# Two layers of product-key experts on one core: a tile's u rows are requested ahead of the preceding tile's v rows

## The reference

```
def peer_ffn(tokens, wq, sub_keys, u, v):
    ...
        best_s, best = lax.top_k(cand_s, PEER_TOPK)
        idx = jnp.take_along_axis(cand_i, best, axis=-1)
        gate = jax.nn.softmax(best_s, axis=-1)
        act = jax.nn.gelu(jnp.einsum('td,thkd->thk', h, u[idx]).astype(F32))
        return jnp.einsum('thk,thkd->td', (gate * act).astype(v.dtype), v[idx])
```

## Time and profile before

| | us |
|---|---|
| median of three timed runs | 2939.14 |
| lowest, highest | 2937.1, 2950.22 |
| the profiled execution, its own time | 2943.2 |
| its span, first to last instruction | 2941.4 |
| full loop of layer 0, PE never idle | 1000 to 1850 |
| outputs of 24 tiles alone, layer 1 | about 2293 to 2358 |
| full loop of layer 1 | about 2367 to 2915 |

### The profile page before, as it was taken

How to read it: one execution, slowest core, us unless ns; L and a number is a source line. 1 busy time by engine, 2 the same in 40 slices (tenths; PEclk the granted TensorE clock), 3 DMA queues, 4 the chain that set the end, 5 groups by cost and what they waited for, 6 DMA issues and landing times. The chain is left out here.

```text
span 2941.4 us, 42761 instructions
## 1 busy us (share of the span) xinstructions
PE 2698.3 (92%) x14782; PEld 2307.4 (78%) x14782; DVE 2279.4 (77%) x4146; ACT 1159.3 (39%) x2016; POOL 849.8 (29%) x565
## 2 busy tenths in 40 slices
PE   7999978899788999999999999789888789999997
PEld 3888863689777899999999999664787578888886
DVE  2788877799997777778787878744898867777778
ACT  2233320433583333333333333223446445555553
POOL 0000001435453244444333333100575412212222
PEclk9999979899999999999999999899989899999999
DMA  6223225314479898888888888320356989888986
GB/s 254 106 81 128 86 87 196 119 63 158 140 218 361 325 328 316 306 308 309 305 313 309 307 305 317 143 79 6 152 172 176 380 304 323 314 314 311 321 317 221
DMA packets 247818, 682.39 MB, mean 232 GB/s; under 512 B 20172, under 2 KB 106804, under 8 KB 244020
## 3 DMA queue, kind: packets, MB, share of 16 engines
q1 hardware_dynamic: 192436, 480.00, 46.2%
q0 software_dynamic: 55296, 201.35, 19.2%
HBM read 635.34 MB, written 45.92 MB: 232 GB/s over the span
## 5 line engine op out<-in xcount | busy, mean ns | idle before, releaser
L1043 PE MATMUL bank<-h_parts,u_hi 128*128 128x384 f32 (+1 forms) x3712 | 801.0, 308 | 43.6 <-DVE u_lo L1984 31.2
L1102 PE MATMUL bank<-v_parts,p_parts 128*128 128x512 f32 x3072 | 747.0, 393 | 8.9 <-DVE p_parts L2009 8.9
L1043 PEld LDWEIGHTS bank<-h_parts,u_hi 128*128 128x128 f32 x3712 | 632.6, 192 | 73.2 <-DVE u_lo L1984 42.3
L1102 PEld LDWEIGHTS bank<-v_parts,p_parts 128*128 128x128 f32 x3072 | 580.0, 189 | 129.3 <-issue 7.3
L1043 PE MATMUL bank<-h_parts,u_lo 128*128 128x384 f32 (+1 forms) x1856 | 571.1, 308 | 0.0
L1984 DVE TENSOR_TENSOR u_lo<-arena,u_hi 128x1024 fp32r<-128x1024 f32 x208 | 254.4, 1223 | 132.3 <-ACT u_hi L1398 121.5
L1043 PEld LDWEIGHTS bank<-h_parts,u_lo 128*128 128x128 f32 x1856 | 356.7, 192 | 0.0
L2007 DVE TENSOR_TENSOR v_parts<-arena,v_parts 128x1024 fp32r<-128x1024 f32 x256 | 313.0, 1223 | 55.1 <-ACT v_parts L1488 53.3
L1398 ACT ACTIVATE u_hi<-arena 128x1024 fp32r<-128x1024 f32 x208 | 219.8, 1057 | 288.2 <-DMA arena<-in_u 288.2
L1488 ACT ACTIVATE v_parts<-arena 128x1024 fp32r<-128x1024 f32 x256 | 269.6, 1053 | 80.9 <-PE bank L1102 60.1
L2271 POOL DMA_INDIRECT arena<-in_v,arena x128 | 198.9, 1554 | 319.0 <-DVE arena L2029 295.2
(11 more groups left out here) (302 smaller groups left out, 4140.8 us busy)
## 6 DMA issues: line engine op xcount, KB each, us to landing
arena<-in_u SPq DMA_DIRECT2D x256, 512.0 KB
arena<-in_v SPq DMA_DIRECT2D x256, 512.0 KB
arena<-in_wm SPq DMA_DIRECT2D x80, 512.0 KB
arena<-in_wst SPq DMA_DIRECT2D x19, 2048.0 KB, 8.1
gate_scratch<-arena SPq DMA_DIRECT2D x18, 2048.0 KB, 8.7
arena<-gate_scratch SPq DMA_DIRECT2D x30, 768.0 KB
arena<-in_whd SPq DMA_DIRECT2D x8, 2560.0 KB, 9.1
arena<-gate_scratch SPq DMA_DIRECT2D x30, 384.0 KB
```

Of the source, the lines that this page charges most:

```text
L1043: last = mm(banks[q][:, 0:ND[p]], w[:, q, col], h[:, k, DS[p]], start=(n3 == 0), stop=(n3 == 3 * KT - 1))
L1102: last = mm(banks[2 + 2 * b + half][:, :], x[:, q, at:at + P], y[:, q, col], start=(first and i == 0), stop=(final and i == 2))
```

## The change

The load of u is taken out of `experts` into `load_u`. `experts` for tile j now first loads u of tile j+1 (if there is one) and then v of tile j. The first one, u of tile K0 + 2 = 26, is issued ahead of the loops, in layer 1 ahead of the layer-norm rows. No load is added or removed, the sizes and each load's own wait stay as they are.

```
+                def load_u(j, q, N):
                     sp.wait_ge(u_l[q], 1 + N)
                     sp.dma_start(u_raw[:, q, :], a["u"][p, j]).then_inc(u_in[q], 16)
+
+                def experts(j, q, N, more=True):
+
+                    if more:
+                        load_u(j + 1, 1 - q, N + q)
                     sp.wait_ge(v_l[q], 1 + N)
                     sp.dma_start(v_raw[:, q, :], a["v"][p, j]).then_inc(v_in[q], 16)
...
+                load_u(K0 + 2, 0, K0 // 2 + 1 + N0)
                 if p == 0:
                     sp.wait_ge(tok_done, 1)
...
-                    experts(j, j % 2, j // 2 + N0)
+                    experts(j, j % 2, j // 2 + N0, j + 1 < NK)
```

More of the change, by code:

```diff
@@ L643, in gates @@
                     sp.dma_start(gin[:, slot, 0:ND[p] // GCH].rearrange("p c h t f -> p (c h t f)"), gd[jb, :, 0:ND[p] * 4]).then_inc(gin_in[slot], 16)
-                def experts(j, q, N):
+                def load_u(j, q, N):
                     sp.wait_ge(u_l[q], 1 + N)
                     sp.dma_start(u_raw[:, q, :], a["u"][p, j]).then_inc(u_in[q], 16)
+                def experts(j, q, N, more=True):
+                    if more:
+                        load_u(j + 1, 1 - q, N + q)
                     sp.wait_ge(v_l[q], 1 + N)
```

## The result

| | us |
|---|---|
| kernel before, median of four runs | 2940.47 |
| changed kernel, median of four runs | 2904.2 (2902.88 to 2905.97) |
| ratio | 0.9869, 95% interval 0.9848 to 0.9889 |
| forecast | 2913, range 2905 to 2930 |

The change makes the kernel 36.3 us faster by the medians, where 26.5 us were forecast. The ratio is the one on record over the runs of both kernels; it is not the quotient of the two medians, which is 0.9877. Its numbers are six higher than before from the expert loops on: L1049 are the scores, L1101 and L1108 the outputs, L1404 and L1990 the copies of u, L1494 and L2013 those of v, L654 the v load.

A forecast was written before the change was run, and what follows sets the result against it. PE was taken to bound layer 0's loop and late u rows layer 1's. 24 us in that loop plus 2.5 us at its start made 26.5 us, off 2939.14: 2912.6, forecast as 2913 us, range 2905 to 2930.

The forecast's parts named there:

- What bounds the kernel: Layer 0's loop is PE-bound; layer 1's waits for late u rows, 5.26 us a tile against 4.96, at most 28.6 us.
- The 85%: Layer 1's loop: 85% of the 28.6 us comes back, 24 us, leaving 4 us for tiles behind gates.
- The cover: Layer 1's loop: u gains between 2.15 and some 4 us, above PE's longest wait of 2.0 us, covering almost every late tile.
- The start of the loop: Start of layer 1's loop: u of tile 26 goes ahead of 1.5 MB, removing PE's idle time; 2.5 us, bounds 0 to 5.
- The low end of the range: Whole kernel: 2905 us, allowing a gain of no more than the full 28.6 + 5 us.
- Why it works: Layer 1's loop: u is issued 2.15 us earlier, and 512 KB of v ahead of it go, at most 1.9 us.
- B: Layer 1's loop: DMA engines become the bound, a tile takes 5.11 us; 2917 to 2932 us, chance 0.22.
- C: Layer 1's loop: DMA stays at 318 GB/s, u's flight grows 2.15 us or more; 2932 to 2942 us, chance 0.10.
- D: Layer 1's loop: v becomes late in u's place and the kernel slower; 2950 to 2985 us, chance 0.04.

The follow-up runs named there:

- layer 0 only: Kernel before with the new load order in layer 0 only, layer 1 as before: 2940.59 us, ratio 0.9996.
- layer 1 only: Kernel before with the new load order in layer 1 only, layer 0 as before: 2903.09 us, ratio 0.9859.
- norm rows first: Changed kernel with layer 0 as before and layer 1's first u load (tile 26) put back behind the three layer-norm loads: 2908.5 us, ratio 0.989.
- without the lead: Changed order in layer 1 only, u ahead of v but still waiting for the same v_lo, layer 0 as before: 2905.63 us, ratio 0.9868.
- the lead is gone and bytes are added: Layer 1 order changed, u still waiting for v_lo, with 128 KB more loaded a tile: 2902.14 us, ratio 0.9864.

## Why the prediction came out short

**What bounds the kernel: right.** Layer 0 had nothing to give (ratio 0.9996 alone), layer 1's loop waited for u, and the gain is there.

**The 85%: this is the step that failed, by its size.** "I take 85% of the 28.6 us, which leaves 4 us for tiles behind gates." Nothing was left: the pace became 4.962 us, PE's own. From tile 28 to 127 the loop went from 99 x 5.253 to 99 x 4.962, 28.8 us in these two profiles; against the second kernel with the old order in layer 1 (5.283) it is 31.8 us. The term was sized 24 and measured 29 to 32.

The discount kept 4 us for the very tiles that held most of the loss: 18.8 of 28.9 us lay in the tiles behind gates, and 0.1 us of it is left. That none of them stays late has a reason that the prediction's own rows of SP's queue showed: the u load that stood right behind the gates went ahead of them. No row stood behind the size of the discount, and the start of each tile, which would have told which tiles were late, was not read.

**The cover: right in its result, too high in its size.** The argument ahead of the discount was that u gains 2.15 to 4 us, more than PE's longest wait of 2.0 us. Counted from the free slot (the end of the u_lo before it in that slot) to the landing, as medians, u of the tiles behind gates came after 9.3 us before and 7.1 us now, 2.2 us sooner. In the other three of four tiles it gained 1.7 (the tile after), 0.1 and 0.6 us: the earlier issue was there, but the flight grew. That was enough, because little was lost in those tiles. In this the forecast was lucky.

**The start of the loop: right in kind, short by 1 us.** 2.5 us were forecast; tile 28 came 106.8 - 103.5 = 3.3 us sooner (the mean of before and layer 0 only, and the mean of the changed kernel twice and layer 1 only). The kernel with norm rows first gives 2 to 3 us of it back.

**Together** the loop from tile 24 on gave 545.6 - 512.3 = 33.3 us (means of the same kernels), against 26.5. The medians differ by 36.3 and 38.9 us in the two comparisons. 33.3 of 2941 is a ratio of 0.9887, at the upper edge of the two intervals (0.9848 to 0.9889, 0.9841 to 0.9886). The two profiled spans differ by 2941.4 - 2901.0 = 40.4 us: 8.5 ahead of layer 1's first output product, 4.1 from there to tile 28, 28.9 from there to tile 127, less 1.1 that the changed kernel loses behind tile 127 (29.0 in place of 27.9 us). Whether the remaining 3 to 6 us of the medians are scatter of the stages ahead, whose length varies by 12 us between executions, or something of how the program is laid out, stays open; it is not layer 0's order.

**The low end of the range** was put at the full bound plus 5 us of the start, off a median of 2939.14. That made 2905.5, with no room for the scatter of the medians themselves, which alone moved the kernel before by 1.3 us from the first reading to the second.

**Why it works: half right.** The prediction said that u gains its earlier issue and the bytes of v. The runs show that the place in the queue does nearly all of it (4.977 without the lead, 4.962 with it), and most of it in the tiles behind gates, of which the prediction's "512 KB of v" says nothing. How much v's place and how much the gates' place is worth stays open. And u's flight did not get shorter, 6.08 us in the tile shown, 6.8 us as a median: with u requested earlier each load takes longer.

**B, the DMA engines as the bound: wrong**, and its reasoning too. They moved 390 GB/s when asked, and PE kept its pace. The Trainium skill's "DMA: Bandwidth & Descriptors", section Specifications, which spoke for B with a limit of about 358 GB/s for one core's HBM traffic, does not describe this trace. The page works that figure out as half of what two cores share; here one core ran the program.

**C, a fixed rate: wrong.** The rate rose from 318 to 338 GB/s, and the median flight of u grew by 1.3 us, where C asked for 2.15 or more.

**D, v in u's place: right to be small.** In the changed kernel ACT does not wait for v rows. It does a little where the lead is gone and bytes are added, 9.7 us, and PE doesn't see it.

## What to carry to other kernels

Where one queue feeds two streams into double buffers, issue first the load that is read first, ahead of the other stream and of side loads such as the gates, and put no wait between it and its own free slot that belongs to the other stream. Here that gave 1.3%, and the new order with u issued only 0.26 us earlier gave nearly all of it. Before you discount a gain, read which tiles carry the loss: here two thirds of it lay in the one of four tiles that the discount took as lost. And bytes that nobody wants yet cost PE 2 to 3 us ahead of the first u load of the loop, and some 3.6 us near its end; behind that first u load they cost nothing that shows.

## What the runs showed of the hardware

The DMA engines moved 390 GB/s over 470 us (two or three 512 KB loads of 4 KB rows in flight, gathered rows beside them) at a busy share of 1.01; a stage at 318 GB/s and a share of 0.89 was therefore at 82% of a rate that they can hold, and not at 89% of the most they can do. And taking 448 KB of 1.67 MB a tile off the queue (rate down to 242 GB/s), with u still behind v and gates, helped less than reordering all of it at 335 GB/s: 5.018 against 4.977 us a tile.
